# Taking the first expert's row selection from expert 0's positions and marks, and moving the low halves of its rows in VectorE's order

## The chip, the cores and the metric

The kernel runs on one core of a Trainium2 chip. The metric is the device time of one execution in microseconds (us); for the kernel before it is the median of three runs. One further execution was recorded by the profiler, and every row below comes from that one.

## What is computed

The reference is a stack of three transformer blocks on 256 tokens of width 1024, all in float32. The part that matters here is the mixture-of-experts layer that closes the second block: a router picks two of eight experts for each token, each expert takes its tokens in blocks of up to 128 rows, multiplies them by its own weights, and the results come back weighted by the gates.

```python
def moe_swiglu(h, w_router, w_gate, w_up, w_down):
    logits = (xt @ w_router).astype(jnp.float32)
    top_logit, top_idx = lax.top_k(logits, TOP_K)      # 2 of 8 experts
    gates = jax.nn.softmax(top_logit, axis=-1)
    order = jnp.argsort(top_idx.reshape(-1))           # tokens grouped by expert
    ...
    ys = lax.map(expert_block, (xs, block_expert))     # swiglu with that expert's weights
    ys = ys * gate_buf[:, None]
    out = jnp.zeros((T + 1, D), ys.dtype).at[tok_buf].add(ys)[:T]
```

## The kernel before

Every engine has one hand-written program, and semaphores set the order between them. A product is made nearly exact by splitting both operands into a high half (written by ScalarE, tiles `wh`, `xh`, `ah`) and a low half (written by VectorE with `rest`, a subtraction; tiles `wl`, `xl`, `al`); TensorE then does three matmuls for one (L1354, L1355 and L1356, whatever calls `exact`). Weights come in units of 1 MB over SyncE's queue into six slots `raw`; ScalarE and VectorE split them into three slots `wh` and `wl`.

The expert layer runs as a loop over blocks, at least 8 and at most 11 of them. Each block has 42 weight units. How many blocks there are is known only at run time: VectorE computes it from the router's result, writes it to the small tile `nbt` (L2501, L2502) and adds 1 twice to the semaphore `moe_plan`. TensorE (L1796, L1797), ScalarE (L1169 to L1171), VectorE itself and SyncE each wait for `moe_plan` at 2 and load the number into a register before they enter or go on in their loops.

Ahead of the loop stands a short serial stretch, in this order:

- TensorE transposes the normalised rows (`ztok`), ScalarE copies them out as `z_tok` (L1161, four copies), because tokens must lie on partitions for the gather.
- VectorE finds the two best experts of each token; `plan_f[:, 0]` holds the marks (16 columns: 2 token tiles by 8 experts, 1 where the token goes to the expert). TensorE sums the marks into running positions and counts (`mcum`, L1777 to L1780). VectorE writes the positions to `plan_f[:, 1]` (L2464), the table `lt8` and the flags `plan_f[:, 4]` (L2467).
- VectorE turns positions into row numbers `kcol` (L2468 to L2477), makes the selection `sel` in four instructions (L2484 twice, `stt` twice), writes the row numbers as integers `kidx` for GpSimd (semaphore `moe_rows`, L2490), and goes on with the plan (L2492 to L2502), the gates and `klast` (L2510).
- TensorE waits for the four `ztok` copies and for both parts of `sel`, then gathers the first block's rows: 32 matmuls with 128 columns (L1786), 16 into each of two PSUM banks (`gather0`, `gather1`). In a trace `z_tok` and `sel` both go by the name `big`, and the low halves of the rows by `xl`.
- ScalarE copies each bank to the high half `xgh` (L1167, semaphore `gather_hi`). VectorE, behind the plan and the gates, writes the low half `xgl` (L2513, reported as L2052) and goes on with `split_after("co3")`, the low half of the third expert unit.
- TensorE waits for `moe_plan`, loads the number of blocks, waits for six banks to be free (L1816), and enters the loop (L1817). Its first unit needs the low half of the first bank, the second unit that of the second.

GpSimd scatters all rows to memory (`x_rows`, L758) behind `moe_rows`, for the blocks after the first.

Of the kernel before, what the change touches and what calls it, by code (L numbers as in the profile page):

```python
# [11 lines left out]
ALU = mybir.AluOpType  # L12
# [7 lines left out]
TT = T // P  # L20
# [45 lines left out]
E = 8  # L66
EFF = 3584
EFT = EFF // P
CAP = 128
# [22 lines left out]
C_IOTA = C_SBM + P  # L92
# [111 lines left out]
MOE_BANK = {use: (b, len(uses), j) for b, uses in MOE_USES.items() for j, use in enumerate(uses)}  # L204
# [19 lines left out]
def build(nc, x_dram, mem_dram, c_dram, cst_dram, cols_dram, main_dram, moe_dram, out):  # L224
    ctx = ExitStack()
    with ctx:
        def sb(name, shape, dt=F32):
            return ctx.enter_context(nc.sbuf_tensor(name, shape, dt))
# [3 lines left out]
        def sem(name):  # L232
            if name not in sems:
                sems[name] = ctx.enter_context(nc.semaphore(name))
            return sems[name]
# [32 lines left out]
        plan_f = sb("plan_f", [P, 16, 16])  # L268
# [13 lines left out]
        kcol = sb("kcol", [P, 2, TT])  # L282
# [6 lines left out]
        def cc(at, n=P):  # L289
            return cst[:, at:at + n]  # L290
# [4 lines left out]
        def flat(t):  # L295
            return t[:, :, :].rearrange("p a b -> p (a b)")

        def view(at, a, b, base=None):
            return (big if base is None else base)[:, at:at + a * b].rearrange("p (a b) -> p a b", a=a)
# [24 lines left out]
        sel = view(5120, TT, CAP)  # L324
# [14 lines left out]
        xgh = flat(xh)[:, 0:KT * CAP].rearrange("p (a b) -> p a b", a=KT)  # L339
        xgl = flat(xl)[:, 0:KT * CAP].rearrange("p (a b) -> p a b", a=KT)  # L340
# [16 lines left out]
        def four_of(t, j):  # L357
            return t[:, 4 * j:4 * j + 4, :].rearrange("p a b -> p (a b)")
# [172 lines left out]
        def bank(name):  # L531
            return ps[:, S.at[name][0], :]

        def claim(pe, name):

            b, _, k = S.at[name]
            if k:
                pe.wait_ge(sem(f"drained{b}"), k)
# [5 lines left out]
        def wait_drained(eng, name):  # L544
            b, _, k = S.at[name]
            eng.wait_ge(sem(f"drained{b}"), k + 1)
# [4 lines left out]
        def drained(name):  # L551
            return sem(f"drained{S.at[name][0]}")
# [1481 lines left out]
        def _(dve):  # L2034
            V = nc.vector
            step = [0]

            def link(ins):

                step[0] += 1  # L2040
                ins.then_inc(sem("dve_step"), 1)
                dve.wait_ge(sem("dve_step"), step[0])

            def stt(out_, in0, scalar, in1, op0, op1):
                return V.scalar_tensor_tensor(out=out_, in0=in0, scalar=scalar, in1=in1, op0=op0, op1=op1)  # L2045
# [4 lines left out]
            def rest(out_, whole, leading):  # L2050

                return V.tensor_tensor(out_, whole, leading.bitcast(F32), ALU.subtract)  # L2052
# [7 lines left out]
            def split_after(name, nb=None):  # L2060

                p = POS[name] + SPL
                if p >= len(SPLIT):
                    return
                if nb is None and p >= POS0:
                    dve.wait_ge(sem("hi_ready"), p + 1)
                    rest(wl[:, p % SPL, :], raw[:, (U0 + p - POS0) % RAW, :],
                         wh[:, p % SPL, :]).then_inc(sem("lo_ready"), 1)
                else:
                    split_lo(p, nb)  # L2070
# [377 lines left out]
            for a in range(2):  # L2448
# [16 lines left out]
            link(stt(lt8[:, :, 0:E], cnt.unsqueeze(1).broadcast_to([P, E, E]), float(CAP),  # L2465
                     cc(C_LT, E * E).rearrange("p (a b) -> p a b", a=E), ALU.is_gt, ALU.mult))
            V.tensor_scalar(plan_f[:, 4, 0:E], cnt, float(CAP), None, ALU.is_gt).then_inc(drained("mcum"), 1)  # L2467
            link(V.tensor_reduce(plan_f[:, 5, 0:E], lt8[:, :, :], AX_X, ALU.add))  # L2468
            two = lambda r: plan_f[:, r, :].rearrange("p (a b) -> p a b", a=TT)
            link(stt(two(9), two(1), float(CAP), plan_f[:, 5, 0:E].unsqueeze(1).broadcast_to([P, TT, E]), ALU.is_ge,  # L2470
# [3 lines left out]
            for a in range(2):  # L2474
# [2 lines left out]
            V.tensor_reduce(kcol[:, :, :].rearrange("p a b -> p (a b)"),  # L2477
                            plan_f[:, 13:15, :].rearrange("p a (b c) -> p (a b) c", b=TT), AX_X,
                            ALU.add).then_inc(sem("moe_keys"), 1)
            iota = cc(C_IOTA, CAP)  # L2480

            dve.wait_ge(sem("moe_keys"), 1)
            for t in range(TT):
                V.tensor_scalar(sel[:, t, :], iota, kcol[:, 0, t:t + 1], None,  # L2484
                                ALU.is_equal).then_inc(sem("sel_half"), 1)
            dve.wait_ge(sem("sel_half"), TT)
            for t in range(TT):
                stt(sel[:, t, :], iota, kcol[:, 1, t:t + 1], sel[:, t, :], ALU.is_equal,
                    ALU.add).then_inc(sem("moe_sel"), 1)
            V.tensor_copy(kidx[:, :, :], kcol[:, :, :]).then_inc(sem("moe_rows"), 1)  # L2490
            wait_drained(dve, "mcum")
            link(stt(plan_f[:, 15, 0:E], plan_f[:, 5, 0:E], float(1 - E), ei, ALU.add, ALU.add))  # L2492
            link(V.tensor_tensor(plan_f[:, 15, 0:E], plan_f[:, 15, 0:E], plan_f[:, 4, 0:E], ALU.add))
# [14 lines left out]
            V.tensor_tensor(gcol[:, 1, :], gcol[:, 0, :], pexp[:, 0:2], ALU.mult).then_inc(sem("moe_gates"), 1)  # L2508
            link(V.tensor_scalar(pexp[:, 9:10], pexp[:, 8:9], -1.0, float(CAP), ALU.add, ALU.mult))
            V.tensor_scalar(klast[:, :, :], kcol[:, :, :], pexp[:, 9:10], None, ALU.subtract).then_inc(sem("moe_last"), 1)  # L2510
            for j in range(2):
                dve.wait_ge(sem("gather_hi"), j + 1)
                rest(four_of(xgl, j), bank(f"gather{j}"),  # L2513
                     four_of(xgh, j)).then_inc(sem(f"moe_drained{MOE_BANK[f'G{j}'][0]}"), 1)
            split_after("co3")
            link(V.tensor_scalar(kept[:, :, :], kcol[:, :, :], pexp[:, 9:10], None, ALU.is_lt))
            V.tensor_tensor(gkept[:, :, :], gcol[:, :, :], kept[:, :, :], ALU.mult).then_inc(sem("moe_kept"), 1)
# [314 lines left out]
```

## Time and profile before

| | |
|---|---|
| median of three runs | 1835.2 us |
| lowest and highest run | 1834.9 and 1836.87 us |
| span of the profiled execution | 1835.6 us |
| TensorE busy | 1801.9 us (98% of the span) |
| VectorE busy | 1405.0 us (77%) |
| ScalarE busy | 1163.9 us (63%) |
| GpSimd busy | 229.4 us (12%) |
| mean DMA rate | 285 GB/s |

The span runs from the first to the last instruction of the profiled execution; it lies 0.4 us above the median of the runs and inside their spread. For TensorE the profile also gives the granted clock, 1.00 being 2.4 GHz and 0.50 being 1.2 GHz. Of TensorE's matmuls the ends are modelled. A name ending in q, as `PEldq`, is an engine's sequencer, which does register and semaphore work. The stretch of the change lies between 509 and 526 us, the expert loop between 522 and 1475 us.

### The profile page before, as it was taken

Reading aid. Unit: us, or ns where it says so; the run is one execution under the profiler, and the core shown is the slowest. Engines: PE = TensorE matmul, PEld = TensorE weight load, DVE = VectorE, ACT = ScalarE, POOL = GpSimd, SP = SyncE. Lnnn points to the kernel's source line nnn. Section 1 sums busy time; section 2 is a strip of 40 time slices with the busy share of each in tenths; the row PEclk is TensorE's granted clock in tenths of the full one; section 3 lists DMA queues with packets and bytes.
Section 4 is the critical chain, followed back from the end, with each engine's and each line's share of the span. In section 5 each row is a group of like instructions: output and inputs, shape, how many; then the busy total and the mean of one; then the engine's idle time right before and its main releaser. Section 6 shows DMA issues by size and latency. Waiting matters only on the chain.

```text
span 1835.6 us, 28123 instructions
## 1 busy us (share of the span) xinstructions
PE 1801.9 (98%) x10836; PEld 1598.3 (87%) x10836; DVE 1405.0 (77%) x1329; ACT 1163.9 (63%) x1149; POOL 229.4 (12%) x194
## 2 busy tenths in 40 slices
PE   8999999999999999999999999999999999899998
PEld 8988999998878888888888888888887899799997
DVE  6665877679678888888889888888889857665553
ACT  6765434457667777777777777777776757543332
POOL 0462111302020000000000000000007011302221
PEclk9999999999989999999999999999999999999998
DMA  9633888831359999999999999999999943235530
GB/s 391 270 122 145 310 333 328 315 138 39 123 223 385 367 393 381 366 399 373 383 385 374 393 374 370 389 375 392 374 367 420 371 161 138 93 115 184 184 138 24
DMA packets 75407, 523.27 MB, mean 285 GB/s; under 512 B 8296, under 2 KB 8448, under 8 KB 14784
## 3 DMA queue, kind: packets, MB, share of 16 engines
q1 hardware_dynamic: 73056, 514.02, 73.4%
q0 software_dynamic: 2272, 8.15, 1.2%
q8 instruction: 56, 0.92, 0.2%
q14 instruction: 23, 0.19, 0.0%
HBM read 506.38 MB, written 15.75 MB: 284 GB/s over the span
## 4 chain that ended last, share of the span: by engine, by line
PE 93%; DVE 4%; ACT 2%; issue 1%; DMA 0%; POOL 0%; DVEq 0%; SPq 0%; ACTq 0%
PE ps L1354 27%; PE ps L1356 27%; PE ps L1355 27%; DVE wl L2052 1%; PE ps L1677 1%; PE ps L1839 1%; PE ps L1384 1%; ACT wh L828 1%; PE ps L1532 1%; DVE big L2045 1%; PE ps L1368 1%; PE ps L1549 1%; PE ps L1488 0%; PE ps L1377 0%; DMA big<-in_mem 0%
## 5 line engine op out<-in xcount | busy, mean ns | idle before, releaser
L2052 DVE TENSOR_TENSOR wl<-raw,wh 128x2048 fp32r<-128x2048 f32 x446 | 1026.2, 2303 | 261.8 <-ACT wh L828 148.5
L1180 ACT ACTIVATE wh<-raw 128x2048 fp32r<-128x2048 f32 x336 | 644.5, 1919 | 181.8 <-PE ps L1356 181.2
L1354 PE MATMUL ps<-wh,xh 128*128 128x512 f32 (+1 forms) x1040 | 396.3, 381 | 1.7 <-DVE wl L2052 1.7
L1356 PE MATMUL ps<-wh,xl 128*128 128x512 f32 (+1 forms) x1040 | 390.0, 375 | 0.0
L1355 PE MATMUL ps<-wl,xh 128*128 128x512 f32 (+1 forms) x1040 | 389.5, 375 | 0.0
L1354 PE MATMUL ps<-xh,wh 128*128 128x256 f32 x1120 | 321.9, 287 | 5.4 <-DVE xl L2052 3.5
L828 ACT ACTIVATE wh<-raw 128x2048 fp32r<-128x2048 f32 x107 | 204.4, 1910 | 178.2 <-PE ps L1356 174.3
L1355 PE MATMUL ps<-xl,wh 128*128 128x256 f32 x1120 | 317.2, 283 | 0.0
L1356 PE MATMUL ps<-xh,wl 128*128 128x256 f32 x1120 | 317.2, 283 | 0.0
L1354 PEld LDWEIGHTS ps<-wh,xh 128*128 128x128 f32 x1040 | 195.8, 188 | 37.9 <-DVE wl L2052 2.9
L1356 PEld LDWEIGHTS ps<-wh,xl 128*128 128x128 f32 x1040 | 195.7, 188 | 35.6
L1355 PEld LDWEIGHTS ps<-wl,xh 128*128 128x128 f32 x1040 | 195.9, 188 | 33.9 <-issue 0.5
L1354 PEld LDWEIGHTS ps<-xh,wh 128*128 128x128 f32 x1120 | 215.4, 192 | 9.3 <-issue 6.0
L1355 PEld LDWEIGHTS ps<-xl,wh 128*128 128x128 f32 x1120 | 215.3, 192 | 0.6 <-issue 0.5
L1356 PEld LDWEIGHTS ps<-xh,wl 128*128 128x128 f32 x1120 | 215.1, 192 | 0.0
L1354 PE MATMUL ps<-wh,ah 128*128 128x512 f32 x448 | 175.8, 392 | 1.1 <-DVE al L2052 1.1
L1356 PE MATMUL ps<-wh,al 128*128 128x512 f32 x448 | 174.6, 390 | 0.0
L1355 PE MATMUL ps<-wl,ah 128*128 128x512 f32 x448 | 174.4, 389 | 0.0
L1354 PE MATMUL ps<-ah,wh 128*128 128x256 f32 x496 | 142.2, 287 | 0.4 <-POOL al L738 0.2
L1355 PE MATMUL ps<-al,wh 128*128 128x256 f32 x496 | 140.7, 284 | 0.0
L1356 PE MATMUL ps<-ah,wl 128*128 128x256 f32 x496 | 140.6, 283 | 0.0
L738 POOL TENSOR_TENSOR al<-att_p,ah 128x512 fp32r<-128x512 f32 x27 | 74.8, 2771 | 337.9 <-ACT ah L1040 337.9
(327 smaller groups left out, 1978.0 us busy)
## 6 DMA issues: line engine op xcount, KB each, us to landing
raw<-in_experts SPq DMA_DIRECT2D x336, 1024.0 KB, 7.0
raw<-in_units SPq DMA_DIRECT2D x134, 1024.0 KB, 5.3
x_rows<-big SPq DMA_DIRECT2D x1, 6144.0 KB, 36.0
big<-x_rows SPq DMA_DIRECT2D x8, 512.0 KB, 7.8
y_rows<-big SPq DMA_DIRECT2D x7, 512.0 KB, 8.5
y_rows<-big SPq DMA_DIRECT2D x1, 2560.0 KB, 41.7
sqz<-gate_rows POOLq DMA_DIRECT2D x12, 192.0 KB, 4.3
big<-in_mem SPq DMA_DIRECT2D x1, 1024.0 KB, 7.1
```

Source lines behind the costliest of these rows:

```text
L738: pool.tensor_tensor(al[:, c % 2, :], sg[:, c % 2, :], ah[:, c % 2, :].bitcast(F32), ALU.subtract).then_inc(sem("hid_lo"), 1)
L828: act.activation(wh[:, p % SPL, :], raw[:, n % RAW, :], ACT.Copy).then_inc(sem("hi_ready"), 1)
L1180: act.activation(wh[:, p % SPL, :], raw[:, n % RAW, :], ACT.Copy).then_inc(sem("hi_ready"), 1)
L1354: mm(out_, lh, rh, start=start, stop=False, **kw)
L1355: mm(out_, lh, rl, start=False, stop=False, **kw)
L1356: return mm(out_, ll, rh, start=False, stop=stop, **kw)
L1368: ins = pe.transpose(bank(name)[:, at:at + P], src, ident)
L1384: ins = mm(bank(f"nsum{k}")[:, t:t + 1], src[:, at:at + P], ones[:, 0:1], start=(c == 0 and t == 0), stop=(c == KT - 1), skip_group_check= ...
L1532: ins = mm(s[:, at:at + nk], m["q"][:, P * t:P * t + P], m["k"][:, 0:nk], start=True, stop=True)
L1549: mm(o, m["v"][0], pT[:, 0:T], start=True, stop=False, skip_group_check=True)
L1677: mm(bank(f"conv{c}")[:, 0:T], diag[:, n % DIAG_RING, :], upad[:, c, tap:tap + T], start=(tap == 0), stop=(n + 1 == taps_through(PE_CONV, ...
L2052: return V.tensor_tensor(out_, whole, leading.bitcast(F32), ALU.subtract)
```

## The change

The selection of the first expert no longer comes from the row numbers. Block 0 is expert 0's, so a token belongs to it where expert 0's mark is 1, in the row that its position says. That is one instruction for each of the two token tiles, comparing the iota with the position and multiplying by the mark, and it stands directly behind the flags `plan_f[:, 4]`. The four instructions that built `sel` from `kcol`, and the wait between them, are gone.

The two instructions that write the low halves of the gathered rows move forward in VectorE's program: the first to just ahead of the integer row numbers `kidx`, the second to just behind them. Both thereby stand ahead of the rest of the plan (`moe_plan`), of the gates and of `klast`. Each keeps its wait for ScalarE's copy (`gather_hi`). No other engine's program changes.

```diff
             V.tensor_scalar(plan_f[:, 4, 0:E], cnt, float(CAP), None, ALU.is_gt).then_inc(drained("mcum"), 1)
+            iota = cc(C_IOTA, CAP)
+            for t in range(TT):
+                V.tensor_scalar(sel[:, t, :], iota, plan_f[:, 1, E * t:E * t + 1], plan_f[:, 0, E * t:E * t + 1],
+                                ALU.is_equal, ALU.mult).then_inc(sem("moe_sel"), 1)
             link(V.tensor_reduce(plan_f[:, 5, 0:E], lt8[:, :, :], AX_X, ALU.add))
...
-            iota = cc(C_IOTA, CAP)
-
+
+            def gathered_rest(j):
+
+                dve.wait_ge(sem("gather_hi"), j + 1)
+                rest(four_of(xgl, j), bank(f"gather{j}"),
+                     four_of(xgh, j)).then_inc(sem(f"moe_drained{MOE_BANK[f'G{j}'][0]}"), 1)
+
+            gathered_rest(0)
             dve.wait_ge(sem("moe_keys"), 1)
-            for t in range(TT):
-                V.tensor_scalar(sel[:, t, :], iota, kcol[:, 0, t:t + 1], None,
-                                ALU.is_equal).then_inc(sem("sel_half"), 1)
-            dve.wait_ge(sem("sel_half"), TT)
-            for t in range(TT):
-                stt(sel[:, t, :], iota, kcol[:, 1, t:t + 1], sel[:, t, :], ALU.is_equal,
-                    ALU.add).then_inc(sem("moe_sel"), 1)
             V.tensor_copy(kidx[:, :, :], kcol[:, :, :]).then_inc(sem("moe_rows"), 1)
+            gathered_rest(1)
             wait_drained(dve, "mcum")
...
             V.tensor_scalar(klast[:, :, :], kcol[:, :, :], pexp[:, 9:10], None, ALU.subtract).then_inc(sem("moe_last"), 1)
-            for j in range(2):
-                dve.wait_ge(sem("gather_hi"), j + 1)
-                rest(four_of(xgl, j), bank(f"gather{j}"),
-                     four_of(xgh, j)).then_inc(sem(f"moe_drained{MOE_BANK[f'G{j}'][0]}"), 1)
             split_after("co3")
```

## Rows read from the trace of the kernel before

**Rows 1.** The page: TensorE's busy time, and its granted clock in 40 slices.

```profile
PE 1801.9 (98%) x10836; PEld 1598.3 (87%) x10836; DVE 1405.0 (77%) x1329; ACT 1163.9 (63%) x1149; POOL 229.4 (12%) x194
PEclk9999999999989999999999999999999999999998
```

**Rows 2.** Chain that ended last, 505 to 560 us: start, us, what.

```profile
514.39 0.62 DVE big L2045 x2
515.25 6.73 PE ps L1786 x32
521.99 0.23 PE ps L1354
```

**Rows 3.** Waits: TensorE's in 505 to 560 us and 520 to 1470 us, SyncE's there.

```profile
PE ps L1786 <- DVE big L2045: 3.2, 1, 3.2
...
PE ps L1354 <- DVE wl L2052: 1.4, 1, 1.4
PE ps L1354 <- DVE al L2052: 1.1, 1, 1.1
...
SPq L614 <- DVE wl L2052: 755.8, 328, 27.3
```

**Rows 4.** VectorE in order of time, 507 to 560 us: start, us, line, operation, tiles.

```profile
512.39 0.17 DVE L2467 TENSOR_SCALAR plan_f<-ps 128x8 f32<-128x8 f32 x1
...
513.87 0.48 DVE L2484 TENSOR_SCALAR big<-cst,kcol 128x128 f32<-128x128 f32 x2
...
514.92 0.16 DVE L2490 CAST kidx<-kcol 128x4 uint32<-128x4 f32 x1
514.99 0.16 DVE L2045 SCALAR_TENSOR_TENSOR plan_f<-plan_f,cst 128x8 f32<-128x8 f32 x1
...
516.44 0.13 DVE L2502 TENSOR_SCALAR nbt<-pexp 1x1 int32<-1x1 f32 x1
...
517.14 0.23 DVE L2510 TENSOR_SCALAR klast<-kcol,pexp 128x4 f32<-128x4 f32 x1
519.67 0.69 DVE L2052 TENSOR_TENSOR xl<-ps,xh 128x512 fp32r<-128x512 f32 x1 [2.30 <-ACT xh L1167]
522.65 0.69 DVE L2052 TENSOR_TENSOR xl<-ps,xh 128x512 fp32r<-128x512 f32 x1 [2.29 <-ACT xh L1167]
523.26 2.28 DVE L2052 TENSOR_TENSOR wl<-raw,wh 128x2048 fp32r<-128x2048 f32 x1
```

**Rows 5.** ScalarE in order of time, 507 to 560 us.

```profile
511.43 2.42 ACT L1161 ACTIVATE big<-ps,rcol 128x512 f32<-128x512 f32 x4 [0.62 <-DVE rcol L2083]
...
519.04 0.60 ACT L1167 ACTIVATE xh<-ps 128x512 fp32r<-128x512 f32 x1 [3.68 <-PE ps L1786]
522.02 0.60 ACT L1167 ACTIVATE xh<-ps 128x512 fp32r<-128x512 f32 x1 [2.38 <-PE ps L1786]
```

**Rows 6.** TensorE's sequencer, lines 1797 and 1817: duration min/median/max ns, starts in us.

```profile
L1797 PEldq TENSOR_LOAD <-nbt x1: 667/667/667, 518.4 to 518.4; - x1
L1817 PEldq FUSED_REGOPS  x1: 50/50/50, 519.8 to 519.8; - x1
```

**Rows 7.** TensorE by stretch: us, busy (matmuls), granted clock, DMA share, GB/s.

```profile
504.32:507.73 3.41, 3.41 (x9) 0.50 0.00 0
...
511.15:514.56 3.41, 0.83 (x6) 1.00 0.00 0
514.56:517.97 3.41, 2.71 (x13) 0.50 0.09 37
517.97:521.39 3.42, 3.42 (x18) 0.50 0.92 365
```

**Rows 8.** The chain in 498 to 509 us, then in 516 to 518 us.

```profile
502.32 0.96 PE ps L1749 x4
...
504.26 3.42 PE ps L1749 x8
...
515.80 2.35 PE ps L1786 x11
```

## The prediction

> **What bounds the kernel now.** I read the page first. TensorE is busy for 98% of the span and nearly always at the full granted clock [rows 1]. That makes it the engine whose lost time reaches the end, unless another engine or the loads hold it back later. Behind the change they don't: in 520 to 1470 us, some 950 us of expert blocks, TensorE waited for VectorE twice, 2.5 us in all, while the loads stood 755.8 us waiting for a free slot [rows 3]. So whatever moves the start of the expert loop moves the end by as much, in either direction.
>
> Next the chain around the change. VectorE's last two selection instructions start at 514.39, the gather runs from 515.25 for 6.73 us (32 matmuls), and the first expert unit follows at 521.99 with no gap [rows 2]. Two things stand out. The selection is what the gather waits for, so a faster one helps. And the gather ran at half clock: the granted clock is 0.50 from 514.56 to 521.39, after a stretch in which TensorE was busy for 0.83 of 3.41 us only [rows 7].
>
> Last, what ends where inside that chain. VectorE finishes the plan at 516.57 (516.44 + 0.13) and then waits for the two `xl` instructions, at 519.67 and 522.65 [rows 4]. TensorE's sequencer loads the number of blocks at 518.4, and has passed L1817 by 519.9 [rows 6]: it runs ahead of the gather's matmuls, so the load costs nothing. The wait for `moe_plan` is free too, for it had been met at 516.57.
>
> **Step 1, the earlier selection.** Before, its two pairs start at 513.87 and end at 515.01. Now two instructions follow L2467, which starts at 512.39 [rows 4]. Two-operand compares of this size took 0.48 us for the pair L2484; the form with two columns as scalars is not in VectorE's rows, and I bound it by that and the 0.62 us of the `stt` pair [rows 2]. The selection is ready at 513.0 to 513.2, 1.8 to 2.0 us sooner. But the gather also needs ScalarE's four `z_tok` copies, which end at 513.85 (511.43 + 2.42) [rows 5]. They become the later wait. With the 0.24 us that lay between the selection and the gather before (515.01 to 515.25) as the upper end and nothing as the lower, the gather starts at 513.85 to 514.1; I take 514.05, **1.2 us sooner**. The two instructions delay `kcol` by 0.5 us and the removed four free 1.1 us behind it; neither is on TensorE's path, since VectorE next waits for the gather.
>
> **Step 2, the gather itself.** At half clock 11 of its matmuls take 2.35 us, 0.21 each. Four router matmuls take 0.96 us at full clock and eight take 3.42 us at half, so full clock costs 0.56 of half [rows 8], 0.12 us for a gather matmul. Bounds: all at half clock, 6.8 us; all at full, 3.8 us. I take the middle: the wait ahead shrinks from 3.2 us [rows 3] to 2.0 but the stretch stays mostly idle, so the clock falls at about the same moment, 514.6; TensorE is then busy without a break. At 504.32 it was, and had its clock back after 3.41 us; at 514.56 it stood idle for the first 0.7 us and the low stretch lasted 6.83 us [rows 7]. So 4 matmuls at full clock, 16 at half (3.4 us), 12 at full: 0.5 + 3.4 + 1.4 = 5.3 us. The gather ends at 519.4, **1.4 us** gained beside the 1.2. Were that all, the kernel would be 2.6 us faster.
>
> **Step 3, the moved low halves.** This is the cost. VectorE works in program order, and `moe_plan` now stands behind both low halves. What is queued behind the second wait: the rest of the plan, `moe_plan`, the gates, `klast`, the low half of the third unit. Who waits for it: TensorE, ScalarE and VectorE at the loop's entry. The second low half can only come when the whole gather has been done and copied: before, the gather's end at 521.98 was followed by the copy at 522.02 [rows 5] and by the subtraction, which ended at 523.34 (522.65 + 0.69), 1.36 us behind the gather. From the first plan instruction behind it to `nbt` it took 514.99 to 516.57, 1.58 us, less 0.08 by which neighbours overlap (514.92 + 0.16 against 514.99) [rows 4]: 1.50 us. Then TensorE loads the number: from 518.4 to the end of L1817 at 519.85 some 1.5 us [rows 6]; with the sequencer's hand-over to the first matmul I put 1.7, an estimate. The load took 0.67 us of that, and it can't run ahead any longer, since what it waits for comes after the gather. So between the last gather matmul and the first expert matmul a gap opens of 1.36 + 1.50 + 1.7 = **4.6 us**, where there was none. Bounds 4.2 (hand-over at nothing, sequencer steps tighter) to 5.0.
>
> Low half 0 costs nothing: it ends 1.7 us behind its bank before (full 16 matmuls of 0.21 us after 515.25, at 518.66; subtraction done at 520.36), and the new gap is far longer. ScalarE's own register load is hidden behind the first unit. `split_after("co3")` (2.28 us) follows `klast`, which started 0.7 us behind the plan's end (517.14) and took 0.23 [rows 4], and is done by about 525.5 (plan at 522.3); the third unit begins two units of 12 matmuls, 0.23 us each [rows 2], after 524.0, at 529.5 at the earliest, so it stays covered. `kidx` slides from 514.92 to about 519, behind low half 0; GpSimd's four scatters wait for it and slide by as much; they, and the selection for the last block behind `klast`, feed nothing before the second block. SyncE's queue is passed by nothing; the slot that the third unit's split frees comes at about the old time.
>
> **Step 4, the clock at the loop's start.** TensorE now stands 4.6 us. After 3.2 us it was at 0.50 [rows 3, 7], so it enters the first unit at 524.0 at half clock. Low stretches lasted 3.41 and 6.83 us [rows 7], and part of this one passes in the gap; I take 4.2 us of unit work at half clock, of which 0.44 is lost (the 0.56 above): 1.85 us, and 0.2 us to fill again. Bounds: 0 to 6.8 us, 0 to 3.0 us lost. **2.0 us**. The Trainium skill ("TensorE: Matmul & The Clock Gate", section "Loop structure matters more than you think") marks a copy out of PSUM by VectorE as not breaking TensorE's warmth. By that rule this step would be nothing and the sum +2.0 instead of +4.0. The fall at 514.56, while TensorE stood waiting for VectorE, speaks against it wherever the next matmul needs what comes of the copy.
>
> **Sum.** −1.2 − 1.4 + 4.6 + 2.0 = +4.0 us on the span of 1835.6, 1839.6. The median lies 0.4 us below that span, so I forecast 1839.2.
>
> **Rivals.** (a) *The clock falls and stays.* It doesn't come back in the gather (+1.5) and the start of the expert sees the longest stretch (+1.0): +6.5, 1841.7. For it: the longer low stretch occurred here. (b) *The clock doesn't fall before the gather*, since it starts 1.2 us sooner: the gather gains 2.9 instead of 1.4, and what is left is +2.5, or +1.0 if the loop's start is also mild: 1836.2 to 1837.7. For it: only 2.0 us of idling are left there. (c) *The copy doesn't cool TensorE*, the page's rule: the gather as forecast, no loss in step 4: +2.0, 1837.2. (d) *Not slower:* TensorE isn't held at L1797, because its read of the number still runs ahead of the matmuls as at 518.4 [rows 6], and the gap stays closed: −2.6, 1832.6. It decides at one point: `moe_plan` would have to come 1.7 us before the gather's end. By the order of VectorE's program it comes 2.86 us behind it, so this needs my reading of the wait to be wrong. (e) *The change doesn't do what it says:* some other wait than the selection holds the gather at 515.25, and steps 3 and 4 alone remain: +6.6, 1841.8. Against it: `z_tok` is ready at 513.85 [rows 5], and the program has no third wait.
>
> **How the numbers follow.** A run of this kernel can be told from no change at about 0.2%, 3.7 us; the line is at 1838.9 and 1831.5. Chances: forecast 0.52 (spread +3.3 to +5, about four fifths above the line), (a) 0.16, (b) 0.18, (c) 0.06, (d) 0.04, (e) 0.04. Slower: 0.42 + 0.16 + 0.04 = 0.62. Within: 0.10 + 0.18 + 0.06 + 0.02 = 0.36. Faster by more than 0.2% only if (d) gains more than worked out: 0.02. For the range, low: (b) at +1.5, 1836.7; high: the upper bounds of steps 2 to 4 together, +7, 1842.2. Both signs of the clock terms lie inside; (d) is left out.
>
> **What would show it.** In the changed profile the gather starts at about 514.0, released by ScalarE L1161 (step 1); the clock is back at 1.00 before it ends at about 519.4 (step 2); TensorE is idle for 4.2 to 5.0 us between L1786 and L1354 with TENSOR_LOAD L1797 inside that gap, and VectorE's order there is `xl`, plan, `nbt` (step 3); the granted clock is 0.50 when the first unit starts (step 4). I am wrong if L1354 follows L1786 without a gap, or if TensorE picks up the lost time inside the blocks.

## The result: 0.36% slower, by a wait that the moved instructions open in front of the expert loop

| | before | after |
|---|---|---|
| median | 1835.05 us (8 runs) | 1840.97 us (8 runs) |
| lowest and highest | 1833.1 and 1837.1 us | 1838.95 and 1846.17 us |
| profiled execution, span | 1835.6 us | 1844.0 us |
| ratio, 95% interval | | 1.0036, 1.0025 to 1.0048 |

The interval is a loss of 4.6 to 8.8 us. The two spans can't simply be subtracted. In every run whose span is on record the time lies about 1.8 us above the span, or a little more. The profiled execution of the changed kernel took 1845.83 us in all and is one of the two longest of its eight runs. By the same 1.8 us that of the kernel before (span 1835.6) took some 1837.4 us, an estimate, about 2.3 above its median; that its span looked only 0.4 us above the median compares two different measures.

Already ahead of the change the changed kernel's execution lay 5.24 us behind that of before: VectorE takes the router's result (L2442) at 514.52 instead of 509.28. On its chain is a transfer of the first block that the change doesn't touch:

```profile
63.09 8.28 DMA sqz<-gate_rows
```

Of the nine traces shown in this document this transfer is on the chain of the two longest only, this one and that of e2 (8.67 us there). In these two VectorE takes the router's result at 514.5 and 514.7, in the other seven at 509.0 to 511.9. I therefore measure from L2442 to the first turn of the loop's hidden rows on TensorE (L1839 in both traces, four matmuls some 30 us later) and call that **the stretch**. First VectorE's row and TensorE's row of before, then the same two of after (orders of time: start, us, engine, line, tiles):

```profile
509.28 0.17 DVE L2442 COPY lg<-ps 128x16 f32<-128x16 f32 x1 [8.95 <-PE ps L1762]
538.41 0.60 PE L1839 MATMUL ps<-cst,att_p 128*128 128x128 f32 x4
...
514.52 0.17 DVE L2442 COPY lg<-ps 128x16 f32<-128x16 f32 x1 [7.31 <-PE ps L1762]
548.68 0.60 PE L1839 MATMUL ps<-cst,att_p 128*128 128x128 f32 x4
```

The stretch took 29.13 us before and 34.16 us after: **5.03 us longer**. On the page hardly anything of it shows: TensorE's share is the same as in [rows 1].

```profile
PE 1804.4 (98%) x10836; PEld 1600.4 (87%) x10836; DVE 1404.2 (76%) x1327; ACT 1164.2 (63%) x1149; POOL 227.6 (12%) x194
```

The chain of the changed kernel through it (start, us, what; L1161 is the `z_tok` copy, L1786 the gather, L1354 the first expert matmul) answers to [rows 2]:

```profile
516.67 2.43 ACT big L1161 x4
519.10 0.44 issue
519.54 5.45 PE ps L1786 x32
525.02 0.61 ACT xh L1167
525.65 0.69 DVE xl L2052
...
527.83 2.09 issue
529.92 0.79 PE ps L1354
530.71 0.43 PE ps L1355
...
534.53 0.23 PE ps L1355
```

Where before the expert followed the gather at once, the chain now leaves TensorE for ScalarE, for VectorE and for 2.09 us of issue. Behind the issue each expert matmul takes 0.43 us until 534.5 and 0.23 from there on.

VectorE in the changed kernel, which answers to [rows 4]. The second `xl` stands ahead of the plan's first instruction (526.26), and `nbt` is written at 527.82:

```profile
517.71 0.59 DVE L2470 TENSOR_SCALAR big<-cst,plan_f 128x128 f32<-128x128 f32 x2
...
522.88 0.69 DVE L2052 TENSOR_TENSOR xl<-ps,xh 128x512 fp32r<-128x512 f32 x1 [3.30 <-ACT xh L1167]
523.49 0.16 DVE L2493 CAST kidx<-kcol 128x4 uint32<-128x4 f32 x1
525.65 0.69 DVE L2052 TENSOR_TENSOR xl<-ps,xh 128x512 fp32r<-128x512 f32 x1 [2.00 <-ACT xh L1167]
526.26 0.16 DVE L2045 SCALAR_TENSOR_TENSOR plan_f<-plan_f,cst 128x8 f32<-128x8 f32 x1
...
527.69 0.13 DVE L2506 TENSOR_SCALAR nbt<-pexp 1x1 int32<-1x1 f32 x1
```

TensorE's sequencer at L1797 (compare [rows 6]) and TensorE's waits in 520 to 1480 us (compare [rows 3]). The load of the number of blocks is now inside the gap, and the gap is the loop's longest wait:

```profile
L1797 PEldq TENSOR_LOAD <-nbt x1: 1064/1064/1064, 527.9 to 527.9; - x1
...
PE ps L1354 <- issue: 4.9, 1, 4.9
PE ps L1354 <- DVE wl L2052: 1.8, 2, 1.4
```

The granted clock by stretch (us, TensorE busy, granted clock, DMA share, GB/s), which answers to [rows 7]. It falls twice now: once a little behind the gather's start, and again in the gap, and stays low into the expert's first matmuls:

```profile
517.31:520.73 3.42, 1.19 (x10) 1.00 0.00 0
520.73:524.14 3.41, 3.41 (x18) 0.50 0.00 0
524.14:527.56 3.42, 0.84 (x7) 1.00 0.38 153
527.56:530.97 3.41, 1.05 (x3) 0.50 0.90 353
530.97:534.38 3.41, 3.41 (x10) 0.50 0.97 327
```

### The profile page after: what moved, and what is told of

It is laid out like the page before. It is cut to its first block, busy times and chain, and to the rows that moved or that the text cites. A ratio compares the mean times of both kernels' runs of the same rounds, so it can differ in the third digit from the quotient of the medians.

```text
span 1844.0 us, 28121 instructions
## 1 busy us (share of the span) xinstructions
PE 1804.4 (98%) x10836; PEld 1600.4 (87%) x10836; DVE 1404.2 (76%) x1327; ACT 1164.2 (63%) x1149; POOL 227.6 (12%) x194
## 4 chain that ended last, share of the span: by engine, by line
PE 91%; DVE 4%; ACT 2%; issue 1%; DMA 1%; POOL 1%; DVEq 0%; SPq 0%; ACTq 0%
PE ps L1354 27%; PE ps L1356 27%; PE ps L1355 27%; PE ps L1677 1%; DVE wl L2052 1%; PE ps L1839 1%; PE ps L1384 1%; ACT wh L828 1%; DVE big L2045 1%; PE ps L1368 1%; PE ps L1549 0%; PE ps L1532 0%; DMA sqz<-gate_rows 0%; PE ps L1377 0%; PE ps L1847 0%
## 5 line engine op out<-in xcount | busy, mean ns | idle before, releaser
L1354 PE MATMUL ps<-wh,xh 128*128 128x512 f32 (+1 forms) x1040 | 397.5, 382 | 7.1 <-issue 4.9
L1355 PE MATMUL ps<-wl,xh 128*128 128x512 f32 (+1 forms) x1040 | 390.3, 375 | 0.0
L1354 PE MATMUL ps<-xh,wh 128*128 128x256 f32 x1120 | 323.4, 289 | 5.9 <-DVE xl L2052 3.5
L1355 PE MATMUL ps<-xl,wh 128*128 128x256 f32 x1120 | 318.2, 284 | 0.0
L1354 PEld LDWEIGHTS ps<-wh,xh 128*128 128x128 f32 x1040 | 196.3, 189 | 44.0 <-issue 6.7
L1355 PEld LDWEIGHTS ps<-wl,xh 128*128 128x128 f32 x1040 | 196.5, 189 | 34.2 <-issue 0.5
L1354 PEld LDWEIGHTS ps<-xh,wh 128*128 128x128 f32 x1120 | 216.4, 193 | 10.2 <-issue 6.7
L1355 PEld LDWEIGHTS ps<-xl,wh 128*128 128x128 f32 x1120 | 216.5, 193 | 0.6 <-issue 0.5
L1354 PE MATMUL ps<-wh,ah 128*128 128x512 f32 x448 | 175.8, 392 | 0.0
L1355 PE MATMUL ps<-wl,ah 128*128 128x512 f32 x448 | 174.5, 389 | 0.0
L1354 PE MATMUL ps<-ah,wh 128*128 128x256 f32 x496 | 142.3, 287 | 0.4 <-POOL al L738 0.2
L1355 PE MATMUL ps<-al,wh 128*128 128x256 f32 x496 | 140.8, 284 | 0.0
```

Of the source, the lines that this page charges most:

```text
L1354: mm(out_, lh, rh, start=start, stop=False, **kw)
L1355: mm(out_, lh, rl, start=False, stop=False, **kw)
```

## The experiments

All times are medians with the interval of the ratio to the kernel before, which ran beside them (1835.57 us in the first four, 1835.08 us in the last three). "Stretch" is the measure from above, from each kernel's own trace, between the same two instructions where line numbers are shifted; one trace each. "Gap" is from the gather's end to the first expert matmul.

| kernel | median us | ratio | stretch us | gather starts behind L2442, lasts | gap us |
|---|---|---|---|---|---|
| before | | | 29.13 | 5.97, 6.73 | 0 |
| after | 1840.97 | 1.0036 (1.0025 to 1.0048) | 34.16 | 5.02, 5.45 | 4.9 |
| e1 selection only | 1834.83 | 0.9991 (0.9983 to 1.0) | 26.82 | 4.93, 5.44 | 0 |
| e2 low halves only | 1841.89 | 1.0039 (1.0026 to 1.0052) | 34.36 | 5.97, 5.45 | 4.7 |
| e3 second low half behind the plan | 1837.03 | 1.0008 (1.0 to 1.0017) | 29.52 | 4.93, 5.44 | 2.5 |
| e4 after, TensorE kept busy | 1840.02 | 1.0025 (1.0015 to 1.0036) | 31.78 | 4.94, 5.44 | 4.7, of it 3.06 spare work |
| e5 e1, busy before the gather | 1833.53 | 0.9988 (0.9977 to 0.9999) | 25.20 | 4.93, 3.81 | 0 |
| e6 e1, earlier rows | 1834.32 | 0.9993 (0.9983 to 1.0002) | 26.53 | 4.21, 5.44 | 0 |
| e7 e5 and e6 together | 1832.85 | 0.9987 (0.9977 to 0.9998) | 25.01 | 4.24, 3.81 | 0.2 |

All eight medians lie higher against the kernel before than the stretches say, by 0.9 us (after) to 2.4 us (e5). The one thing that all eight comparisons share is the single trace of before, which was of a long execution; so the stretches are best compared with one another, and the gains against 29.13 are probably too large.

**Theory:** the early selection gains; the loss comes from the second low half standing ahead of `moe_plan`, as a wait and, behind the wait, as a lower clock. **Rivals:** the early selection itself costs something; any moved low half costs the same; the slow first unit is a cold loop and not the clock.

### e1: the selection alone

```diff
             V.tensor_scalar(plan_f[:, 4, 0:E], cnt, float(CAP), None, ALU.is_gt).then_inc(drained("mcum"), 1)
+            for t in range(TT):
+                V.tensor_scalar(sel[:, t, :], iota, plan_f[:, 1, E * t:E * t + 1], plan_f[:, 0, E * t:E * t + 1],
+                                ALU.is_equal, ALU.mult).then_inc(sem("moe_sel"), 1)
...
-            (the four instructions that made sel from kcol)
```

> The selection comes from expert 0's positions and marks behind the counts; the low halves of the rows stay where they were, behind the plan. Theory (the loss is the plan that waits for the second low half): the gather starts about 1 us sooner than before, measured from VectorE's first router copy (L2442), the first expert matmul follows the gather without a gap, and the time is 1.0 to 3.5 us below the kernel before, the larger end if the clock comes back during the gather. Rival (the early selection itself costs, through the clock that falls at another moment): a time above the kernel before by 1 us or more, with no gap.

The stretch fell to 26.82 us, 2.3 below before, without a gap. The chain of e1, to be read beside that of after:

```profile
514.07 2.44 ACT big L1161 x4
516.51 0.35 issue
516.86 5.44 PE ps L1786 x32
522.30 0.24 PE ps L1354
522.54 0.23 PE ps L1355
```

The median is 0.7 us lower and the interval's upper end is 1.0, so in the whole time the gain is at the edge of what can be told, and below the 1.0 to 3.5 us that I had put. The trace shows the earlier start clearly; how much of the 2.3 us belongs to the selection is taken up in step 2 below. The rival falls: the selection costs nothing.

### e2: the low halves alone

```diff
             (the old selection, from kcol)
+            gathered_rest(0)
             V.tensor_copy(kidx[:, :, :], kcol[:, :, :]).then_inc(sem("moe_rows"), 1)
+            gathered_rest(1)
...
-            (both low halves behind klast)
```

> The old selection from the row numbers; only the low halves of the rows are moved, as in the change. Theory: the same gap of about 4.9 us between gather and first expert matmul as in the changed kernel, and no early start, so 6 to 8 us above the kernel before, 1 to 2 us slower than the changed kernel. Rival (both parts are needed for the loss): within 2 us of the kernel before.

6.3 us above the kernel before, with the gap and no early start. TensorE's two waits in 509 to 540 us are the old one and the new one together:

```profile
PE ps L1354 <- issue: 4.7, 1, 4.7
PE ps L1786 <- DVE big L2045: 3.2, 1, 3.2
```

So the moved low halves alone make the whole loss. I had put e2 1 to 2 us behind the changed kernel; it was 0.9 us by the medians and 0.2 in the stretch. The gather starts 0.95 us later, but the register load was quicker (0.66 us instead of 1.06), and the clock was low for less of the expert's work: 3.41 us instead of 4.46. One thing more I had not expected: the gather starts as late as before (5.97 us behind L2442) and yet lasts 5.45 us, not 6.73. The low clock in the gather, then at the expert's start (531.37 is 0.6 us behind the first expert matmul):

```profile
521.13:524.54 3.41, 3.41 (x19) 0.50 0.00 0
...
531.37:534.78 3.41, 3.41 (x10) 0.50 0.59 178
```

More on the gather below.

### e3: only the second low half moved behind the plan

```diff
             gathered_rest(0)
             dve.wait_ge(sem("moe_keys"), 1)
             V.tensor_copy(kidx[:, :, :], kcol[:, :, :]).then_inc(sem("moe_rows"), 1)
-            gathered_rest(1)
...
             V.tensor_scalar(nbt[0:1, 1:2], pexp[0:1, 8:9], -1.0, None, ALU.add).then_inc(sem("moe_plan"), 1)
+            gathered_rest(1)
```

> The changed kernel, but the second low half stands directly behind moe_plan instead of ahead of it; the first stays early. Theory: only the second one holds the plan up behind the end of the gather. The first is done about 1.7 us behind its bank, so the plan is there some 1.5 us later, near the gather's end; the gap shrinks from 4.9 to 1 to 2 us and the time lies within 2 us of the kernel before. Rival (any low half ahead of the plan costs the same): still 3 us or more above.

Of the changed kernel's loss, 5.9 us in the medians and 5.0 in the stretch, 4.5 and 4.6 are gone. The 1.5 us that are left in the medians lie within the 2 us that I had put. But the gap was 2.5 us, above what I had put. The chain shows why: the plan still waits for the first bank, which is full at 518.5, and the register load follows (the 1.52 us of issue):

```profile
515.03 3.46 PE ps L1786 x16
518.51 0.60 ACT xh L1167
519.14 0.69 DVE xl L2052
...
521.41 1.52 issue
522.92 0.49 PE ps L1354
```

The first low half isn't free either, then: alone it leaves 2.7 us of stretch against e1. The expert's matmuls ran at 0.23 us in e3; the clock didn't fall in that gap, so the clock's share of the loss is gone with the second low half.

### e4: the changed kernel with TensorE kept busy

```diff
                 gather(bank(f"gather{j}"), j).then_inc(filled(f"gather{j}"), 1)
+            keep_running("idle_gap", 28)
             pe.wait_ge(sem("moe_plan"), 2)
```

> The changed kernel, with 28 extra 128-column transposes into an idle bank behind the gather (some 3.4 us at full clock), so that TensorE works through most of the gap. Theory: the wait stays (first expert matmul at the same distance behind the plan) but the clock is at 1.00 when the first unit starts, and the stretch from L2442 to the first L1839 is 1.5 to 2.5 us shorter than in the changed kernel (34.2 us there). Rival (the slow first unit is not the clock's but the cold start of the loop, its instructions or its loads): no shorter.

The wait stayed and the clock didn't fall. The chain of e4 (its lines are one higher: L1787 is the gather, L1489 the added transposes, L1355 the first expert matmul), then TensorE by stretch, clock in the third place:

```profile
514.12 5.44 PE ps L1787 x32
519.55 3.06 PE ps L1489 x28
522.61 1.64 issue
524.25 0.49 PE ps L1355
...
519.60:524.20 4.60, 3.01 (x28) 1.00 0.57 228
524.20:534.00 9.80, 9.75 (x43) 1.00 0.74 247
```

The first unit begins 4.7 us behind the gather, nearly as in the changed kernel (4.9), and the stretch is 2.4 us shorter. Of that 0.3 us lies ahead of the first expert matmul, for the register load took 0.70 us instead of 1.06. Behind it are 2.05 us (16.71 from there to L1839, against 18.76), and they are the clock's. This parts the loss: wait and clock. The rival of a cold loop falls but for 0.26 us: the first matmul took 0.49 instead of 0.23 us at the full clock too. In the whole time the gain is 0.95 us by the medians and 2.0 by the ratios, and the intervals of after and e4 overlap; the split rests on the traces. The spare work is transposes, and the Trainium skill ("TensorE: Matmul & The Clock Gate", section "Part 4: PE-mode transpose") says that the full clock does not engage for transpose mode. The rows list the spare work as MATMUL and don't tell its mode; if it is that mode, the trace does not agree where the clock is already full, for it stayed at 1.00 through 28 of them and a 1.64 us wait.

### e5, e6, e7: what the gather still waits for

```diff
 e5 and e7, TensorE, behind the three mcum products:
+            keep_running("idle_sel", 14)
 e6 and e7, VectorE:
+            root_by_token(4)
             ei = cc(C_EI, E)
             wait_filled(dve, "lgT")
...
             link(V.tensor_tensor(pexp[:, 0:2].unsqueeze(2), mx8[:, :, 1:2], mx8[:, :, 0:1], ALU.subtract))
-            root_by_token(4)
```

> The selection alone moved (as in e1_selection_only), with 14 extra 128-column transposes into an idle bank between the counts and the gather, so that TensorE isn't idle for most of the 2 us there. Theory (the gather's half clock comes from TensorE waiting ahead of it): the clock stays at 1.00, the gather takes 3.7 us instead of 5.44, and the stretch from L2442 to the first L1839 falls from 26.8 to about 25.3 us; 3 to 4.5 us below the kernel before. Rival (the gather is slow for its own sake, its 128 columns or its operands): 5.4 us again, no shorter stretch.

Chain and clock of e5 (L1788 is the gather):

```profile
511.14 2.43 ACT big L1162 x4
513.57 0.35 issue
513.93 3.81 PE ps L1788 x32
517.74 0.23 PE ps L1355
...
509.00:514.00 5.00, 4.35 (x37) 1.00 0.01 2
514.00:518.00 4.00, 4.00 (x34) 1.00 0.30 121
```

The gather takes 3.81 us at full clock, and the stretch is 1.6 us shorter than in e1, as expected. The whole time is not: it lies 1.6 us below the kernel before, where I had put 3 to 4.5, and can't be told from e1's.

> The selection alone moved, and VectorE takes the root (root_by_token(4)) ahead of the router's result instead of behind the marks, so that ScalarE's z_tok copies can start sooner. Theory (behind the earlier selection z_tok is the later wait): z_tok ends 0.5 to 0.6 us sooner, and the gather starts 0.5 to 0.7 us sooner than in e1_selection_only (4.3 to 4.4 us behind L2442 instead of 4.94). Rival (the gather waits for the selection or for its own semaphores): it starts no sooner.

The rows end 3.85 us behind L2442 (L2443 here) instead of 4.57, and the gather starts 0.72 us sooner, at 4.21, a little more than I had put: `z_tok` is the later wait. But the stretch gains only 0.3 us. The half clock still lasts until 8.85 us behind L2442 (8.66 in e1), so most of what starts sooner is done at half speed.

> Both additions of e5 and e6 on top of the early selection, low halves in their old place. Theory: the gains add, the stretch from L2442 to the first L1839 is 24.5 to 25.2 us, 4.5 us below the kernel before. Rival (TensorE's load of the number of blocks becomes the late one, since the gather now ends before it): a gap of 0.3 us or more between gather and first expert matmul, and e7 no faster than e5.

The stretch is 25.01 us, 4.1 below before and 0.2 below e5; a gap of 0.2 us is there, for the first low half of the rows rather than for the register load. e7 has the lowest median of all, 1832.85 us, 0.13% below the kernel before (0.02 to 0.23%), 2.2 us and not the 4.5 that I had put; from e5 and e1 it can't be told apart by its median.

## Why the prediction was right, and where it was off

The forecast was 1839.2 us, slower; 1840.97 us was measured, 5.9 us above the kernel before instead of 4.0. The mechanism came as described, and the four signs that the prediction asked for are in the rows above. Step by step, within the stretch:

| step | forecast | measured in after | off |
|---|---|---|---|
| 1, gather starts | −1.2 us | −0.95 (5.97 to 5.02) | +0.25 |
| 2, gather's length | −1.4 us | −1.3 (6.73 to 5.45) | +0.1 |
| 3, gap | +4.6 us | +4.9 (524.99 to 529.92) | +0.3 |
| 4, clock at the loop's start | +2.0 us | +2.3 (the rest of 5.03) | +0.3 |
| sum | +4.0 us | +5.0 | +1.0 |

**Step 1** named the right next wait: the selection is ready at 518.30 (517.71 + 0.59), `z_tok` at 519.09, and e6 moved the gather by moving `z_tok`. Too low was the way from the last copy to the first matmul: 0.44 us, where I took 0.20 (0.35 in e1 and e3 to e6). In the program three more semaphore waits stand behind that of the last copy, also for free banks, which the prediction's "no third wait" passes over; that they make the difference is my guess, and no run shows it.

**Step 2** came out in size, but its reason was only half of it. I tied the shorter half-clock stretch to the gather being under way when the clock falls, and the traces fit that: in before the clock fell 0.7 us ahead of the gather's start and was low for 6.83 us; in the other six traces in which it fell there (after, e1, e2, e3, e4 and e6) it fell 0.3 to 1.2 us behind the start and was low for 3.41 us. But whether it falls ahead or behind isn't set by the change alone: e2 has the gather where before had it and got the short one, since the clock fell later, 6.4 instead of 5.3 us behind L2442. So some of the 1.3 us is luck of the execution, and how much the change has of it in the mean stays open. The medians speak for a small share: e1 gained 0.7 us where its stretch says 2.3, and the changed kernel lost 5.9 where its stretch says 5.0. If the kernel before usually has the short low stretch, the step's −1.4 should have been about nothing, and the rest of the sum, +5.4, comes nearer to the measured 5.9. That is an argument from nine single traces, not shown.

**Step 3** is the main cause, and each piece of it stands in the rows: gather's end to second low half 1.35 us (forecast 1.36), plan 1.48 us (1.50), entry into the loop 2.10 us (1.7). The entry was mis-sized: the load took 1.06 us instead of 0.67. e2 shows that the moved instructions do it without the selection, e3 that the second costs most, e1 that without them the gap is nothing. I was wrong on one cover. "Low half 0 costs nothing" holds only in the shadow of the second; by itself it costs 2.7 us of stretch (e3 against e1), because the plan that stands behind it then ends after the gather.

**Step 4**: the clock was low for 4.46 us of expert work (529.92 to 534.38) against 4.2 forecast, and a matmul cost 0.43 instead of 0.23 us, 0.47 of it lost where the router's smaller ones gave 0.44. The first took 0.79 us. e4 takes the low clock away and leaves the wait: 2.05 us for the clock, forecast 1.85; the other 0.3 is the slow first matmul, forecast 0.2. In e2 the clock fell only 0.6 us behind the first expert matmul, after a gap of 4.7 us, and all 3.41 us of its low stretch lay on expert work; in the changed kernel it fell 2.6 us into the gap. Rival (c), that the wait for the copy doesn't cool TensorE, would have given 1837.2; the trace and e4 decide against it here. What it took from the Trainium skill ("TensorE: Matmul & The Clock Gate", section "Loop structure matters more than you think") stands there for matmuls that follow at once, and here they came 4.9 us later.

**The rivals.** (a) is not what happened in this trace, for the clock came back in the gather; at the loop's start the longer low stretch did come (6.83 us), but 2.4 us of it passed in the gap, so it cost 2.3 us and not 3.0. (b) fell: the clock fell all the same, only 1.2 us behind the gather's start, and the gather wasn't done at full clock. (d) fell with the load at 527.9, inside the gap, and (e) with the gather starting 0.95 us sooner.

**Beyond the stretch** the profile gives something back: from L1839 to the end the changed kernel's trace is 1.9 us shorter (10.27 us behind there, 8.4 at the end). At the end of the expert loop the clock was at 0.50 for 6.83 us before, and stayed full in after. Both rows are of 1480 to 1500 us, before first; the clock is the number behind the bracket:

```profile
1480.00:1500.00 20.00, 19.98 (x139) 0.83 0.13 52
...
1480.00:1500.00 20.00, 18.22 (x129) 1.00 0.60 226
```

I had no term for that, and it doesn't seem to belong to the change. From L1839 to the end before's trace took 1297.2 us and each of the other eight 1294.5 to 1295.9, among them e1 and e2, which have only one half of the change each; e5 had the 6.83 us of low clock too and is among the shortest. So before's trace was the long one. Nor was the lost time picked up inside the blocks, as [rows 3] had let expect: from L1839 to the end the changed kernel and e1 took the same, 1295.3 and 1295.4 us.

## What to carry to other kernels

In an engine that works in program order, an instruction that waits for another engine takes everything behind it along. Before such an instruction is moved forward, list what it is moved past, and look among that for a flag that other engines wait for at a loop's entry: here the number of blocks, free as long as it came before the gather's end. And when an earlier step puts a wait in place of work on TensorE, price the wait twice, once as time and once as the clock that it takes from the work behind; a few spare transposes tell the two apart. Ahead of the gather they won 1.6 us of the stretch, too little for the medians of e1 and e5 to show. And before a gain is read from one trace of each kernel, see in more of them whether the old kernel's clock usually falls there: here that was worth 1.3 us, as much as the step itself.

## What the runs showed of the hardware that I had not expected

- A register load from the small tile took TensorE 0.49 to 1.10 us in these traces (0.67 before, 1.06 in after, 1.10 in e1, 0.66 in e2, 0.70 in e4, 0.49 in the others), for the same 4 bytes. With the register steps and waits behind it, the way from the plan's last write to the first expert matmul was 2.1 us in after, 1.7 in e2 and e4 and 1.5 in e3.
- The same gather of 32 matmuls took 6.73, 5.44 or 3.81 us. The granted clock accounts for nearly all of it: with 6.14 and 3.41 us at half clock counted at 0.56, the first two come to 4.0 us each (an estimate).
- 28 spare transposes took 3.06 us, and the clock outlasted them and 1.64 us of waiting; in the changed kernel it fell 2.6 us into the gap without them. In e2 it fell 5.2 us behind the gap's start, and in e3 it outlasted 2.5 us of idling.
